# A two-block transformer on one core: the router's chain before the expert layer written in another order

## The chip, the cores and the metric

The kernel runs on one core of a Trainium2 chip, in one launch. The metric is device time in microseconds (us), the median of several executions. Below, PE is TensorE, DVE is VectorE, ACT is ScalarE, POOL is GpSimd and SP is SyncE, whose queue issues the weight transfers.

## What is computed

Two transformer blocks over 256 tokens of width 1024, in float32. The change lies in the first block's last layer, a hierarchical mixture of 16 experts in 4 groups:

```python
p_group = softmax(tf @ w_rg + b_rg); g_val, g_idx = top_k(p_group, 1)
in_group = e_logits[its group]; e_val, e_idx = top_k(in_group, 2)
weights = g_val * softmax(e_val)
for e in range(N_EXPERTS):
    hidden = silu(t @ w_gate[e]) * (t @ w_up[e])
    y = y + gate[:, e] * (hidden @ w_down[e])
```

Here t is the normed token. The second block then modulates its norms with shifts and scales that are products of a 1024 x 6144 matrix with a vector (w_mod); these products are the "modulation tiles" below.

## The kernel before, in words

Every float32 product is made of three float32r matmuls: a value is held as a high part (its float32r copy) and a low part (what the copy left out), and high x high, low x high and high x low are added up in PSUM. Weights come from HBM as pieces of 128 x 1024 (512 KB), in one long stream that SP issues in order into a ring of four slots (later in the layer four side slots as well). For each piece ACT copies the high part (wh, line 734, function split), DVE subtracts it (wl, line 2020), and PE waits for the low part (semaphore w_lo). SP issues a piece when DVE is done with the one that held its slot. Every engine runs its own list in the order written; nothing is scheduled.

The expert layer starts with the routing chain. PE makes the 20 logits (few_rows), DVE scales them and adds the bias (lines 2281, 2282), PE turns them (turn_logits, line 1566), and DVE finds each token's group (line 2312 to 2318, semaphore rt_group). PE counts the tokens of each group (rt_count), ranks them (rt_rank) and turns the norm's roots (rt_root); one semaphore, rt_counted, stands for all three. From the counts DVE finds the leading group (line 2334 and on) and writes the address of its weights (first_i, semaphore moe_first); SP reads it and only then issues the layer's first weights. DVE goes on with the two best experts, each token's place in its group's queue (dest, line 2358) and the weights of the gates (rt_gate, line 2371). Meanwhile PE turns the tokens themselves, to have them by token (turn_tokens): per chunk of 128 x 512, eight matmuls against the identity add high and low part in one PSUM bank; ACT copies the bank as uh (line 918), and DVE later subtracts uh from the bank to get ul (line 2376, turned_rest). At the end of this part PE multiplies ones, eight times (spin, line 1299, turn_over): it keeps PE busy and leaves no result that is used.

The leading group's four experts then run over all 256 tokens as eight half experts ("unit" jobs, functions gate_up and down: 24 matmuls of 128 x 256 for each of gate, up and down); the other three groups run over at most 128 gathered tokens each, twelve experts ("crowd" jobs, 36 matmuls of 128 x 512 each). The list SEQ mixes them: units 0 to 3 are jobs 0 to 3, then four times three crowd jobs and a unit, so that units are also jobs 7, 11, 15 and 19. In the loop over jobs PE first makes the next job's gate and up, then this job's down product. The first unit also waits for the squares of the context rows' norm (norm("ctx")), the gates (gate_full, gate_set), the clearing of the four sum banks (moe_cleared) and the slots of the crowd tokens (spread_slots).

Six modulation tiles, each two DVE operations of 128 x 1024 (mod_tiles, line 2148), are spread over the units 1 to 6 (MOD_UNIT), that is jobs 1, 2, 3, 7, 11 and 15: each stands ahead of the low part of that unit's hidden values (hidl, line 2440), which the down product waits for. POOL loads the matrix tiles, two ahead. What stands on DVE between the gates' weights and the first low part of weights is this:

```python
for c in range(4):
    turned_rest(c)
add_squares("ctx", 512)
```

## Time and profile before

| | |
|---|---|
| median of 3 executions | 1562.03 us (1559.44 to 1562.79) |
| the profiled execution | 1556.72 us, span 1554.9 us |
| PE busy | 1473.3 us, 95% of the span |
| DVE, ACT busy | 1058.3 us (68%), 758.5 us (49%) |
| mean granted TensorE clock | 0.989 |
| weight transfers | 512 KB a piece, HBM 163 GB/s over the span |

The span is the time from the first to the last instruction of the profiled execution; its own time has 1.8 us around it. PE is busy nearly throughout, so what an edit is worth has to be read from the places where PE stands still.

### The profile page before, as it was taken

The page shows a single profiled execution, that of the slowest core. Times are in us where ns is not written, and L with a number is a line of the kernel's source. Part 1 is how long each engine was busy: PE and PEld are TensorE (multiplying, and loading weights), DVE is VectorE, ACT ScalarE, POOL GpSimd, SP SyncE. Part 2 cuts the span into 40 slices and gives each one's busy share as a digit, 9 for nine tenths or more (in the row PEclk, how much of TensorE's full clock was granted, in tenths as well). Part 3 has the DMA queues.
Part 4 walks back from the last instruction along what each step waited for, and adds up shares of the span by engine and source line. Part 5 has one row for each costly group of instructions (what it writes and reads, how often), then busy time and mean ns, then how long its engine had stood idle before and what let it go on. Part 6 is the DMA issues. An engine that isn't in the chain of part 4 may idle for free.

```text
span 1554.9 us, 24439 instructions
## 1 busy us (share of the span) xinstructions
PE 1473.3 (95%) x8792; PEld 1261.4 (81%) x8792; DVE 1058.3 (68%) x1805; ACT 758.5 (49%) x1293; POOL 94.0 (6%) x167
## 2 busy tenths in 40 slices
PE   7999999699998999997999999999999998999997
PEld 7999698698777877655878888888877966899997
DVE  5877496668888899258687765554579736665554
ACT  5544554346666635346435421443235546574562
POOL 0010000000000000003001100000000002000000
PEclk9999999899999999999999999999999999999999
DMA  8676263249987435403336764555433331356562
GB/s 322 219 272 188 81 187 112 84 148 332 318 284 242 127 120 189 114 14 69 133 114 208 248 203 148 170 194 163 150 124 111 121 94 29 99 173 189 176 185 85
DMA packets 87123, 254.22 MB, mean 163 GB/s; under 512 B 7904, under 2 KB 31600, under 8 KB 86912
## 3 DMA queue, kind: packets, MB, share of 16 engines
q1 hardware_dynamic: 69264, 188.70, 36.8%
q0 software_dynamic: 17776, 64.41, 14.0%
q8 instruction: 53, 0.87, 0.2%
q14 instruction: 30, 0.25, 0.0%
HBM read 251.99 MB, written 1.09 MB: 163 GB/s over the span
## 4 chain that ended last, share of the span: by engine, by line
PE 82%; DVE 10%; ACT 3%; issue 3%; DMA 1%; SPq 0%; DVEq 0%; ACTq 0%
PE pair L1255 80%; DVE wl L2020 1%; DVE sq L2679 1%; PE pair L1299 1%; ACT wh L734 1%; DVE uv L2056 1%; DVE sq L2096 1%; DVE small L2088 1%; PE pair L1444 1%; DMA uv<-in_w_stream 1%; ACT wh L724 0%; DVE spent L2148 0%; DVE uh_f L2148 0%; ACT sq L796 0%; DMA table<-in_table 0%
## 5 line engine op out<-in xcount | busy, mean ns | idle before, releaser
L1255 PE MATMUL pair<-uh,wh 128*128 128x256 f32 (+3 forms) x1280 | 415.8, 325 | 5.4 <-DVE ul L2047 2.8
L1255 PE MATMUL pair<-ul,wh 128*128 128x256 f32 (+3 forms) x1280 | 412.3, 322 | 0.0
L1255 PE MATMUL pair<-uh,wl 128*128 128x256 f32 (+3 forms) x1280 | 411.2, 321 | 0.0
L2020 DVE TENSOR_TENSOR wl<-ring,wh 128x1024 fp32r<-128x1024 f32 x190 | 229.5, 1221 | 58.5 <-ACT wh L734 55.3
L1255 PEld LDWEIGHTS pair<-uh,wh 128*128 128x128 f32 (+1 forms) x1280 | 235.2, 184 | 32.6 <-issue 6.8
L1255 PEld LDWEIGHTS pair<-uh,wl 128*128 128x128 f32 (+1 forms) x1280 | 235.3, 184 | 23.4
L1255 PEld LDWEIGHTS pair<-ul,wh 128*128 128x128 f32 (+1 forms) x1280 | 235.1, 184 | 22.3
L734 ACT ACTIVATE wh<-ring 128x1024 fp32r<-128x1024 f32 x186 | 193.7, 1053 | 81.2 <-PE pair L1255 61.8
L2013 DVE TENSOR_TENSOR wl<-ring,wh 128x1024 fp32r<-128x1024 f32 x120 | 146.8, 1224 | 108.3 <-ACT wh L724 105.0
L724 ACT ACTIVATE wh<-ring 128x1024 fp32r<-128x1024 f32 x124 | 130.4, 1052 | 158.8 <-PE pair L1255 158.8
L1255 PE MATMUL pair<-hh,wh 128*128 128x512 f32 (+1 forms) x512 | 172.5, 337 | 1.8 <-DVE res L2856 1.8
L1255 PE MATMUL pair<-hl,wh 128*128 128x512 f32 (+1 forms) x512 | 172.2, 336 | 0.0
L1255 PE MATMUL pair<-hh,wl 128*128 128x512 f32 (+1 forms) x512 | 170.7, 333 | 0.0
L1255 PEld LDWEIGHTS pair<-hh,wh 128*128 128x128 f32 x512 | 96.1, 188 | 14.2 <-issue 2.5
L1255 PEld LDWEIGHTS pair<-hh,wl 128*128 128x128 f32 x512 | 96.2, 188 | 10.8
L1255 PEld LDWEIGHTS pair<-hl,wh 128*128 128x128 f32 x512 | 96.0, 188 | 9.5
L1209 ACT ACTIVATE sq<-pair 128x512 f32<-128x512 f32 (+1 forms) x64 | 31.3, 489 | 107.4 <-PE pair L1255 105.6
L2821 DVE TENSOR_TENSOR hl<-sq,hh 128x512 f32 (+1 forms) x64 | 35.7, 558 | 69.5 <-ACT hh L1214 69.5
L2133 DVE CUSTOM_DVE_ANT_0 mod_w<-mod_w,mod_c 128x1024 f32<-128x1024 f32 x56 | 68.3, 1220 | 0.0
L640 POOL DMA_DIRECT2D mod_w<-in_mods x67 | 35.4, 529 | 477.4 <-DVE macc L2133 313.9
L1255 PE MATMUL pair<-wh,uh 128*128 128x256 f32 (+1 forms) x192 | 57.5, 300 | 3.0 <-ACT qkp L1042 3.0
L1255 PE MATMUL pair<-wh,ul 128*128 128x256 f32 (+1 forms) x192 | 57.4, 299 | 0.0
(384 smaller groups left out, 2545.5 us busy)
## 6 DMA issues: line engine op xcount, KB each, us to landing
ring<-in_w_stream SPq DMA_DIRECT2D x310, 512.0 KB, 4.3
mod_w<-in_mods POOLq DMA_DIRECT2D x67, 512.0 KB, 3.9
uh_side<-in_w_stream SPq DMA_DIRECT2D x20, 512.0 KB, 5.9
uv<-in_w_stream SPq DMA_DIRECT2D x20, 512.0 KB, 5.8
uh_f<-in_mods POOLq DMA_DIRECT2D x18, 512.0 KB, 4.9
qk_w<-in_mods POOLq DMA_DIRECT2D x6, 512.0 KB, 6.4
in_w<-in_mods POOLq DMA_DIRECT2D x5, 512.0 KB, 3.9
uv<-c_rows POOLq DMA_DIRECT2D x4, 512.0 KB, 7.6
```

Source lines behind the costliest of these rows:

```text
L640: pool.dma_start(dst, src).then_inc(S(f"mod_in{g % 2}"), 16)
L724: act.activation(wh[:, s, :], ring[:, s, :], ACT.Copy).then_inc(S("w_hi"), 1)
L734: act.activation(part_of(wh, n), staged(n), ACT.Copy).then_inc(S("w_hi"), 1)
L1209: act.activation(r, bank[(b0 + j) % 4][:, 0:n], ACT.Relu).then_inc(S("job_emptied_act"), 1)
L1255: ins = pe.matmul(*operands, **flags)
L1299: pe.matmul(bank[b], spin[:, 0:P], spin[:, :], start=True, stop=True)
L1444: last = pe.transpose(bank[6][:, to * P:(to + 1) * P], prob[i % 2][:, j * P:(j + 1) * P], ident)
L2013: tt(wl[:, s, :], ring[:, s, :], wh[:, s, :].bitcast(F32), ALU.subtract).then_inc(S("w_lo"), 1)
L2020: tt(part_of(wl, n), staged(n), part_of(wh, n).bitcast(F32), ALU.subtract).then_inc(S("w_lo"), 1)
L2056: last = stt(o, src, g, r, ALU.mult, ALU.mult)
L2133: return dve.tensor_tensor_reduce(out=mod_w[l][k], in0=mod_w[l][k], in1=mod_c[l][which], scale=1.0, scalar=0.0, op0=ALU.mult, op1=ALU.add, ...
L2821: tt(hl[:, d, 0:n].rearrange("p a b -> p (a b)"), sq[:, 2 + j % 2, 0:n], hh[:, d, 0:n].rearrange("p a b -> p (a b)").bitcast(F32), ALU.sub ...
```

## The change

The routing chain is written in another order, and two things are computed otherwise:

- DVE does the constants (count_up, route, a zeroed tile, the modulation's sums) before it waits for the logits.
- The tokens are turned as eight chunks, four of the high part and four of the low part, with four matmuls each; ACT copies all eight out of PSUM as uh and ul. DVE's subtraction (turned_rest) is gone.
- PE counts the groups ahead of chunk 3; rt_counted stands for the counts alone, and ranks and roots get a semaphore of their own (rt_ranked). PE's spin has 12 matmuls and stands behind the ranks.
- ACT makes the first weight piece's high part ahead of the context's last square; DVE adds the squares and makes the first low part right behind dest, ahead of the gates' weights. PE does norm("ctx") ahead of the first unit.
- The gates are scaled by the root while they are still one value a token, and ACT copies them out of PSUM; DVE multiplied them by the root before. The clearing of the sum banks moves behind spread_slots.
- The six modulation tiles stand in jobs 1, 3, 5, 9, 13 and 17 (MOD_JOBS): two units, and one crowd job out of each three; each stands behind the low part hidl of its job.

```diff
@@ -126 +126 @@
-MOE_SPIN = 8
+MOE_SPIN = 12
@@ -220,2 +220,2 @@
-MOD_UNIT = (0, 1, 1, 1, 1, 1, 1, 0)
-MOD_IN = MOD_MOE + sum(MOD_UNIT)
+MOD_JOBS = (1, 3, 5, 9, 13, 17)
+MOD_IN = MOD_MOE + len(MOD_JOBS)
@@ -443 +443,2 @@
-        turn_banks = [bank[JOBS.number("moe_y", 0) % 4], bank[JOBS.number("moe_y", 1) % 4], bank[6], bank[7]]
+        turn_banks = [bank[JOBS.number("moe_y", j) % 4] for j in range(3)] + [bank[6], bank[7], bank[5], bank[4]]
+        turn_banks.append(turn_banks[0])
@@ -916 +917 @@
-for c in range(4):
+for c in range(8):
@@ -918,2 +919,2 @@
-    act.activation(tok_chunk(uh, c), turn_banks[c][:, :].rearrange("p (a t) -> p a t", a=2),
-                   ACT.Copy).then_inc(S("turned_hi"), 1)
+    act.activation(tok_chunk(uh if c < 4 else ul, c % 4), turn_banks[c][:, :].rearrange("p (a t) -> p a t", a=2),
+                   ACT.Copy).then_inc(S("turned"), 1)
@@ -929 +929,0 @@
-square("ctx", 3, res[:, 6:8, CTX], P, 512)
@@ -931 +931,2 @@
-split(S_MOE + 2)
+split(S_MOE)
+square("ctx", 3, res[:, 6:8, CTX], P, 512)
@@ -933 +934 @@
-split(S_MOE + 4)
+split(S_MOE + 2)
@@ -951,0 +953,6 @@
+        if i == 0:
+            act.wait_ge(S("gate_full"), 1)
+            for j in range(2):
+                act.activation(gates[:, 2 * j:2 * j + 2, :], gate_banks[j][:, :].rearrange("p (a t) -> p a t", a=2),
+                               ACT.Copy).then_inc(S("gate_set"), 1)
+            split(S_MOE + 3)
@@ -955 +962 @@
-        split(last + 3 if i else 0)
+        split(last + 3)
@@ -1572 +1579 @@
-    if c == 3:
+    if c == 4:
@@ -1573,0 +1581,2 @@
+    if c == 7:
+        pe.wait_ge(S("turned"), 1)
@@ -1575,4 +1584,3 @@
-        f, tok = 4 * (c % 2) + j, slice(c // 2 * P, c // 2 * P + P)
-        o = turn_banks[c][:, j * P:(j + 1) * P]
-        mm(o, fh[:, f, tok], ident_r[:, :], start=True, stop=False)
-        last = mm(o, fl[:, f, tok], ident_r[:, :], start=False, stop=True)
+        f, tok = 4 * (c % 2) + j, slice(c % 4 // 2 * P, c % 4 // 2 * P + P)
+        last = mm(turn_banks[c][:, j * P:(j + 1) * P], (fh if c < 4 else fl)[:, f, tok], ident_r[:, :],
+                  start=True, stop=True)
@@ -1585 +1592,0 @@
-turn_tokens(3)
@@ -1589 +1596,5 @@
-    mm(rt_count, tab("nones"), ones_g[:, b, :], start=(b == 0), stop=(b == 1))
+    last = mm(rt_count, tab("nones"), ones_g[:, b, :], start=(b == 0), stop=(b == 1))
+last.then_inc(S("rt_counted"), 1)
+for c in range(3, 8):
+    turn_tokens(c)
+pe.wait_ge(S("moe_first"), 1)
@@ -1595,2 +1606,3 @@
-last.then_inc(S("rt_counted"), 1)
-turn_over(MOE_SPIN, 5)
+last.then_inc(S("rt_ranked"), 1)
+pe.wait_ge(S("turned"), 2)
+turn_over(MOE_SPIN, JOBS.number("moe_y", 1) % 4)
@@ -1627,0 +1640,2 @@
+pe.wait_ge(S("turned"), 8)
+norm("ctx", P, T)
@@ -1630,2 +1643,0 @@
-pe.wait_ge(S("turned_lo"), 4)
-norm("ctx", P, T)
@@ -1638,6 +1650,10 @@
-pe.wait_ge(S("moe_zero"), 1)
-pe.wait_ge(S("gate_set"), 1)
-for b in y_banks:
-    for k in range(2):
-        mm(b[:, k * T:(k + 1) * T], hidl[:, 1, 0:P], uh[:, k, LAT], start=(k == 0), stop=False,
-           skip_group_check=True).then_inc(S("moe_cleared"), 1)
+
+def clear_sums():
+
+    pe.wait_ge(S("moe_zero"), 1)
+    pe.wait_ge(S("gate_set"), 2)
+    for b in y_banks:
+        for k in range(2):
+            mm(b[:, k * T:(k + 1) * T], hidl[:, 1, 0:P], uh[:, k, LAT], start=(k == 0), stop=False,
+               skip_group_check=True).then_inc(S("moe_cleared"), 1)
+
@@ -1710,0 +1727 @@
+        clear_sums()
@@ -2279,4 +2295,0 @@
-dve.wait_ge(S("rt_logits"), 1)
-dve.wait_ge(S("norm_rstd"), NORM["ffn"] + 1)
-ch.link(tt(logit_rows[0:20, :], rt_bank[0:20, 0:T], rstd[0:20, 0:T], ALU.mult))
-ts(logit_rows[0:20, :], logit_rows[0:20, :], tab("b_route", 20), None, ALU.add).then_inc(S("rt_rows"), 1)
@@ -2290 +2303,13 @@
-
+ts(hidl[:, 1, 0:P], ones, 0.0, None, ALU.mult).then_inc(S("moe_zero"), 1)
+ts(eps2, tab("eps"), EPS, None, ALU.mult).then_inc(S("eps2_set"), 1)
+dve.wait_ge(S("mod_used"), MOD_MOE)
+ch.link(tt(modv[:, 0:32], modv[:, 0:32], tab("b_mod")[:, 0:32], ALU.add))
+ch.link(stt(gmod[:, 0, :], modv[:, 16:32], 1.0, tab("g1_0"), ALU.add, ALU.mult))
+ch.link(tt(gcomb.rearrange("p (k o) -> p k o", o=1),
+           gmod[:, 0, :].rearrange("p (k o) -> p k o", o=2)[:, :, 0:1],
+           tab("g_fin1").rearrange("p (k o) -> p k o", o=1), ALU.mult))
+dve.memset(modv[:, 2 * N_MOD:4 * N_MOD], 0.0).then_inc(S("macc_out"), 1)
+dve.wait_ge(S("rt_logits"), 1)
+dve.wait_ge(S("norm_rstd"), NORM["ffn"] + 1)
+ch.link(tt(logit_rows[0:20, :], rt_bank[0:20, 0:T], rstd[0:20, 0:T], ALU.mult))
+ts(logit_rows[0:20, :], logit_rows[0:20, :], tab("b_route", 20), None, ALU.add).then_inc(S("rt_rows"), 1)
@@ -2353,0 +2379 @@
+dve.wait_ge(S("rt_ranked"), 1)
@@ -2358,0 +2385,3 @@
+add_squares("ctx", 512)
+lo_end[0] = N_PIECES
+split(S_MOE)
@@ -2367 +2396 @@
-tt(tok_v[:, :, 0:4], tmp, over(root_of), ALU.mult)
+tt(tok_v[:, :, 0:4], tmp, over(root_of), ALU.mult).then_inc(S("tok_v"), 1)
@@ -2371,13 +2400,2 @@
-tt(lead_w, tmp, over(lone), ALU.mult).then_inc(S("rt_gate"), 1)
-
-def turned_rest(c):
-
-    dve.wait_ge(S("turned_hi"), c + 1)
-    tt(tok_chunk(ul, c), turn_banks[c][:, :].rearrange("p (a t) -> p a t", a=2),
-       tok_chunk(uh, c).bitcast(F32), ALU.subtract).then_inc(S("turned_lo"), 1)
-
-for c in range(4):
-    turned_rest(c)
-add_squares("ctx", 512)
-ts(hidl[:, 1, 0:P], ones, 0.0, None, ALU.mult).then_inc(S("moe_zero"), 1)
-lo_end[0] = N_PIECES
+dve.wait_ge(S("tok_v"), 1)
+tt(lead_w, tok_v[:, :, 0:4], over(lone), ALU.mult).then_inc(S("rt_gate"), 1)
@@ -2384,0 +2403,4 @@
+for b in range(TB):
+    last = ts(pick[:, b, :], count_up[:, :], dest[:, b, :], None, ALU.is_equal)
+last.then_inc(S("pick_set"), 1)
+split(S_MOE + 2)
@@ -2391,22 +2412,0 @@
-ts(eps2, tab("eps"), EPS, None, ALU.mult).then_inc(S("eps2_set"), 1)
-dve.wait_ge(S("mod_used"), MOD_MOE)
-ch.link(tt(modv[:, 0:32], modv[:, 0:32], tab("b_mod")[:, 0:32], ALU.add))
-ch.link(stt(gmod[:, 0, :], modv[:, 16:32], 1.0, tab("g1_0"), ALU.add, ALU.mult))
-ch.link(tt(gcomb.rearrange("p (k o) -> p k o", o=1),
-           gmod[:, 0, :].rearrange("p (k o) -> p k o", o=2)[:, :, 0:1],
-           tab("g_fin1").rearrange("p (k o) -> p k o", o=1), ALU.mult))
-dve.memset(modv[:, 2 * N_MOD:4 * N_MOD], 0.0).then_inc(S("macc_out"), 1)
-split(S_MOE + 2)
-scale_gate(0)
-dve.wait_ge(S("gate_full"), 1)
-for j in range(2):
-    last = tt(gates[:, 2 * j:2 * j + 2, :], gate_banks[j][:, :].rearrange("p (a t) -> p a t", a=2),
-              rstd[:, 0:T].rearrange("p (a t) -> p a t", a=1).to_broadcast([P, 2, T]), ALU.mult)
-last.then_inc(S("gate_set"), 1)
-for b in range(TB):
-    last = ts(pick[:, b, :], count_up[:, :], dest[:, b, :], None, ALU.is_equal)
-last.then_inc(S("pick_set"), 1)
-split(S_MOE + 4)
-dve.wait_ge(S("gate_set"), 1)
-dve.wait_ge(S("moe_cleared"), 8)
-
@@ -2427,3 +2427,2 @@
-        if i:
-            scale_gate(i)
-            split(last + 2)
+        scale_gate(i)
+        split(last + 2)
@@ -2430,0 +2430,2 @@
+        if i == 0:
+            dve.wait_ge(S("gate_set"), 2)
@@ -2435,0 +2437,2 @@
+        if i == 1:
+            dve.wait_ge(S("moe_cleared"), 8)
@@ -2438 +2440,0 @@
-        mod_tiles(MOD_UNIT[n], spent[:, :, :])
@@ -2440,0 +2443 @@
+        mod_tiles(int(i in MOD_JOBS), spent[:, :, :])
@@ -2461,0 +2465 @@
+    mod_tiles(int(i in MOD_JOBS), spent[:, :, :])
```

How it moves PE's list, from the turned logits to the first weights (pair is PSUM, fh and fl are the tokens' parts, small holds the groups, sq the context's squares). Before:

```order
L1566 MATMUL pair<-table,logit_rows 128x20 [waits rt_rows]
...
L1255 MATMUL pair<-ident_r,fh 128x128 [waits norm_rstd]
...
L1255 MATMUL pair<-small,table 128x4 [waits rt_group]
L1255 MATMUL pair<-small,table 128x4 x4
L1255 MATMUL pair<-table,rstd 128x1 x2
L1299 MATMUL pair<-spin 128x512 x8
L1255 MATMUL pair<-fh,wh 128x256 [waits w_lo]
```

and now:

```order
L1573 MATMUL pair<-table,logit_rows 128x20 [waits rt_rows]
...
L1262 MATMUL pair<-small,table 128x4 [waits rt_group]
...
L1262 MATMUL pair<-ident_r,fl 128x128 [waits norm_rstd]
...
L1262 MATMUL pair<-small,table 128x4 [waits moe_first]
L1262 MATMUL pair<-small,table 128x4 x2
L1262 MATMUL pair<-table,rstd 128x1 x2
L1306 MATMUL pair<-spin 128x512 [waits turned]
L1306 MATMUL pair<-spin 128x512 x11
L1262 MATMUL pair<-sq,table 128x256 [waits norm_add,turned]
...
L1262 MATMUL pair<-fh,wh 128x256 [waits w_lo]
```

The two count matmuls stand ahead of most of the turning, the ranks behind it, and the context's norm (sq) stands ahead of the first weights.

DVE's list from dest (the reduce into route) to the first low part of weights. Before:

```order
L2358 TENSOR_REDUCE route<-route 128x2 [waits dve_step]
L2360 SCALAR_TENSOR_TENSOR small<-small 128x2 [waits rt_exp]
...
L2371 TENSOR_TENSOR route<-small,route 128x8 [waits dve_step]
L2376 TENSOR_TENSOR ul<-pair,uh 128x2x256 [waits turned_hi] x4
L2034 TENSOR_TENSOR sq<-sq 128x512 [waits norm_sq]
...
L2020 TENSOR_TENSOR wl<-ring,wh 128x1024 [waits w_hi] x2
```

and now:

```order
L2384 TENSOR_REDUCE route<-route 128x2 [waits dve_step]
L2051 TENSOR_TENSOR sq<-sq 128x512 [waits norm_sq,dve_step]
L2051 TENSOR_TENSOR sq<-sq 128x512 [waits norm_add,norm_sq]
L2037 TENSOR_TENSOR wl<-ring,wh 128x1024 [waits w_hi]
L2389 SCALAR_TENSOR_TENSOR small<-small 128x2 [waits rt_exp]
...
L2401 TENSOR_TENSOR route<-route 128x8 [waits tok_v,dve_step]
```

The gates' weights moved behind the first piece, and the subtraction into ul is not there any more.

DVE's list in job 5, a crowd job, from the low part of its hidden values. Now:

```order
L2464 TENSOR_TENSOR hidl<-pair,hidh 128x256 [waits crowd_hi]
L2165 ISA spent,modv<-uh_f_123,uv 128x1024 [waits mod_used,mod_in0]
...
L2165 ISA uh_f_123,modv<-uh_f_123,uv 128x4x256
...
L2037 TENSOR_TENSOR wl<-uh_side,wh 128x1024 [waits w_hi]
```

A modulation tile (the two ISA rows) stands between hidl and the next low part of weights, where nothing stood before.

## Rows read from the trace of the kernel before

**Rows 1.** The page's chain that ended last, by engine.
```profile
PE 82%; DVE 10%; ACT 3%; issue 3%; DMA 1%; SPq 0%; DVEq 0%; ACTq 0%
```
**Rows 2.** Timeline of PE in routing: start, us, engine, line, instruction, count [idle before].
```profile
291.35 1.23 PE L1255 MATMUL pair<-small,table 128*128 128x4 f32 x10
...
292.88 2.10 PE L1299 MATMUL pair<-spin 128*128 128x512 f32 x8
306.02 0.58 PE L1255 MATMUL pair<-fh,wh 128*128 128x256 f32 x1 [11.04 <-DVE wl L2020]
...
314.01 1.89 PE L1255 MATMUL pair<-sq,table 128*128 128x256 f32 x8
315.74 1.95 PE L1255 MATMUL pair<-table,route 128*128 128x128 f32 x16
319.16 1.19 PE L1255 MATMUL pair<-uh,hidl 128*128 128x256 f32 x8 [1.47 <-DVE gates L2403]
...
325.63 0.60 PE L1255 MATMUL pair<-table,route 128*128 128x128 f32 x4
```
**Rows 3.** Stretches of 1 us: PE, PEld, DVE, ACT, POOL busy; clock; DMA share; GB/s.
```profile
297.00:298.00 1.00, 0.00 (x0) 0.00 (x0) 0.86 (x5) 0.00 (x0) 0.00 (x0) 0.68 0.93 377
309.00:310.00 1.00, 1.00 (x6) 1.00 (x6) 0.00 (x0) 0.00 (x0) 0.00 (x0) 0.50 0.94 340
```
**Rows 4.** Timeline of DVE in the routing chain.
```profile
287.98 0.41 DVE L2281 TENSOR_TENSOR logit_rows<-pair,rstd 20x256 f32<-20x256 f32 x1 [3.20 <-ACT rstd L767]
...
289.92 0.19 DVE L2312 COPY small<-pair 128x40 f32<-128x40 f32 x1
...
290.94 0.17 DVE L2318 TENSOR_TENSOR small<-small 128x8 f32<-128x8 f32 x1
...
293.06 0.16 DVE L2334 TENSOR_REDUCE route<-pair 128x1 f32<-128x4 f32 x1 [1.22 <-PE pair L1255]
...
298.26 0.16 DVE L2358 TENSOR_REDUCE route<-route 128x2 f32<-128x8 f32 x1
...
299.96 2.48 DVE L2376 TENSOR_TENSOR ul<-pair,uh 128x512 fp32r<-128x512 f32 x4
302.36 1.48 DVE L2034 TENSOR_TENSOR sq<-sq 128x512 f32<-128x512 f32 x2
```
**Rows 5.** Timeline of ACT and of SP's queue there, and the transfers' landing times.
```profile
289.34 1.06 ACT L918 ACTIVATE uh<-pair 128x512 fp32r<-128x512 f32 x2
...
303.13 0.63 ACT L754 ACTIVATE sq<-res 128x512 f32<-128x512 f32 x1 [6.20 <-DVE sq L2034]
...
295.02 34.40 SPq L606 DMA_DIRECT2D ring<-in_w_stream  x11
...
DMA to landing us min/median/max: 3.5/4.3/6.8
```
**Rows 6.** Timelines of DVE, ACT and PE in job 7, a unit with a tile.
```profile
389.61 1.22 DVE L2148 CUSTOM_DVE_ANT_1 spent<-uh_f,uv 128x1024 f32<-128x1024 f32 x1
...
390.05 1.04 ACT L734 ACTIVATE wh<-ring 128x1024 fp32r<-128x1024 f32 x1
...
393.51 0.50 PE L1255 MATMUL pair<-wh,xgh 128*128 128x512 f32 x1 [2.43 <-DVE wl L2020]
```
**Rows 7.** Timelines of DVE and PE in the crowd jobs 9 and 13.
```profile
414.33 2.35 DVE L2020 TENSOR_TENSOR wl<-ring,wh 128x1024 fp32r<-128x1024 f32 x2
...
416.49 0.39 PE L1255 MATMUL pair<-wh,hidh 128*128 128x512 f32 x1
...
450.99 0.42 DVE L2461 TENSOR_TENSOR hidl<-pair,hidh 128x256 fp32r<-128x256 f32 x1
...
454.07 0.40 PE L1255 MATMUL pair<-wh,hidh 128*128 128x512 f32 x1
```
**Rows 8.** Who waited for whom, 320 to 500 us: total, times, longest.
```profile
SPq L606 <- DVE wl L2020: 117.1, 79, 11.3
...
ACT wh L734 <- DMA ring<-in_w_stream: 4.0, 6, 3.0
```

More of the change, by code:

```diff
@@ L928, in _ @@
             ch.link(act.activation(gsum, gsum, ACT.Exp, scale=0.5))
+            hi_end[0] = N_PIECES
+            split(S_MOE)
             square("ctx", 3, res[:, 6:8, CTX], P, 512)
-            hi_end[0] = N_PIECES
+            root("ctx", P, T, D, rstd[:, T:2 * T])
             split(S_MOE + 2)
-            root("ctx", P, T, D, rstd[:, T:2 * T])
-            split(S_MOE + 4)
             def gathered(f):
```

## The prediction

> **What bounds the kernel now.** I read the chain that ended last first: PE makes up 82% of it, DVE 10% [rows 1]. PE is the bound, and time is to be found only where PE stands still or runs slowly. So next I went through the timeline of PE for its idle places. Two lie in the routing part [rows 2]: after the last spin matmul, at 294.98, PE does nothing for 11.04 us until the first weights' low part (wl) is there at 306.02, and it waits 1.47 us for the gates at 319.16. The clock comes on top: the granted clock falls during that idle stretch, between 297 and 298, where its mean is 0.68 (2.4 GHz, then 1.2), and at 309, with PE busy again, it still stands at 0.50, 1.2 GHz [rows 3]. The 48 matmuls of the first unit take 7.99 us (306.02 to 314.01); the next unit's 48, from 320.2 to 325.63, take 5.43 [rows 2]. The slow clock thus costs 2.5 us. Third, I followed DVE back from 306.02 [rows 4]: the counts arrive at 293.06, after a wait of 1.22; dest is done at 298.42; the gates' weights follow; then the four subtractions into ul (2.48 us) and the two additions of squares (1.48 us). ACT's last square of the context had waited 6.20 us for these additions and stands ahead of the first weight copy [rows 5]. The weights had been on their way since 295.02 and were no longer the last thing waited for.
>
> Later there are three waits of the kind at 393.51: PE stands 2.43 us for a low part in job 7, and DVE spends two operations of 1.14 on a modulation tile just ahead of it [rows 6]. The trace has this pattern three times, in jobs 7, 11 and 15.
>
> **The routing part, worked forward.** All times are on the trace's clock.
>
> Counts. PE's first two chunks now take 8 matmuls of 0.11 us in place of 16, so PE is free when the logit rows are ready. These start at 287.98 [rows 4]; with 0.41 for each of two such operations and about 0.35 for the two transposes and their landing (an estimate: the counting matmuls take 0.22 each, 1.53 us for seven between 291.35 and 292.88 [rows 2]) the copy starts at 289.15, against 289.92 behind the constants: 0.77 earlier. The constants themselves move into DVE's wait of 3.20 us ahead of the logits; they add up to some 2.4 us and cost nothing there. If that cover were short, each 0.2 us too much would delay all that follows. The group is known at 290.94 + 0.17 - 0.77 = 290.34, two counting matmuls take 0.44, and with 0.2 for the landing the counts are there at 291.0. DVE itself is done with what stands ahead of them at 293.06 - 1.22 - 0.77 = 291.07. The counts are thus read at 291.1, 1.96 us earlier.
>
> Weights. SP's first issue moves with it from 295.02 to 293.06, and with the shortest landing of 3.5 us [rows 5] the first piece is there at 296.56. ACT must have its eight copies behind it: 0.53 each from 289.34 [rows 5] with a short wait for PE's counts, done at 294.1, and the exponentials until 295.7. It makes the high part from 296.6 to 297.65 (1.04 [rows 6]) and then the square (0.63 [rows 5]) until 298.3.
>
> DVE. dest is done at 298.42 - 1.96 = 296.46, the squares are added by 297.95, and the first low part takes 1.22 more, until 299.2. The 2.48 us of subtraction are gone; ACT's four added copies are 2.1 us, and they are over before the landing, which covers them.
>
> PE. After the counts, 20 turning matmuls until 293.05, five small ones until 294.15, twelve spins of 0.26 until 297.3. The context's norm starts at 297.95, when the squares are added, and takes 315.74 - 314.01 = 1.73 us: 299.7. The gap of 0.65 us ahead of it is far shorter than the idle time of over 2 us before the clock fell [rows 2, 3], so I take 2.4 GHz. The first half of the unit ends at 299.7 + 2.72 = 302.4 (24 of the 48 in 5.43). Its second piece is late next: ACT does the norm's root before it (two operations, taken as 0.9 with their landing), then high part 1.05 and low part 1.22, 303.1; PE waits 0.7 and ends at 305.8. The gates' matmuls take 1.85 [rows 2], until 307.65; the next unit's first half until 310.4. Its second piece now stands on ACT behind the two copies of the gates (0.53 each, from 307.85): high part at 310.0, low part at 311.25, a new wait of 0.85. PE gets to spread_slots at 314.0 where it was at 325.63 [rows 2]. The clearing, 1.03 us, comes after it now. **The routing part gives 11.6 - 1.0 = 10.6 us.** All later issues of weights hang on DVE's low parts (SP waited 117.1 us for them, ACT 4.0 us for ring transfers [rows 8]), so the later stages move along.
>
> **The modulation tiles.** In jobs 7, 11 and 15 the low part PE waits for could start when its high part is ready, 390.05 + 1.04 = 391.1, in place of 392.24 behind the tile [rows 6]. That gives 1.12 each, 3.4 us; the rest of the wait stays, as ACT and DVE still hand the values to and fro. In the crowd jobs DVE has less room. In job 9 the tile takes the place of the low part at 414.33: that one then starts at 416.61 and is done at 417.83, while PE wants it at 416.49: a new wait of 1.4 us [rows 7]. In job 13 hidl is issued at 450.99; 0.34 + 2.28 + 1.22 later it is 454.83, and PE wants it at 454.07: 0.8 us [rows 7]. I take job 5, where the transfers run close, like job 9 and job 17 like job 13: 4.4 us for the four. In job 3 DVE now waits for ACT's copy before the tile, 0.5 us that the tile covered before. **The tiles cost 4.4 + 0.5 - 3.4 = 1.5 us.** Bounds: nothing new to wait for (a gain of 3.4) and all four paid in full (4 x 2.28 + 0.5 - 3.4, a loss of 6.2). I take the worked value, which lies nearest to the two jobs read.
>
> **Sum.** -10.6 + 1.5 = -9.1 us. The profiled execution took 1556.72 us with a span of 1554.9, so a like one would take 1547.6. The median of the runs is 5.3 us above the profiled execution; on that scale it is 1562.03 - 9.1 = 1552.9. A measurement here tells a difference from none at about 0.2%, 3.1 us.
>
> **Rivals.**
> 1. *The tiles are paid in full.* DVE has six low parts of 1.22 in each crowd job, so a delay may not be made up before the next unit. Against it: in jobs 9 and 13 DVE is 0.9 and 1.4 us ahead of PE [rows 7]. -10.6 + 6.2 = -4.4: 1557.6.
> 2. *The tiles are hidden*, because PE's wait in one job gives DVE room in the next: -14.0, 1548.0. The two jobs in rows 7 speak against it.
> 3. *The clock falls all the same.* The spin ends at 297.3, and a slip of the squares or the landing lengthens the gap. Price: 2.5 us less the 0.7 wait it swallows: 1554.7.
> 4. *The counts don't come earlier*, so the change doesn't do what it says: SP reads the address a whole 1 us after it is written, and if that or the landing sets the start, PE begins at 301.1, 1.4 us later: 1554.3.
> 5. *The transfers take over, and it is slower.* SP issues strictly in order behind DVE's low parts [rows 8]; a tile in a crowd job holds SP for 2.28 us, just where three jobs in four want six pieces each. It decides when less than 2.28 us of transfers are queued at that moment. Then each tile is lost to the stream, 9.1 us; the stream's start gains only the 1.96 of the first issue, PE's other gains end in waits for transfers, and one modulation load moves from the units into the crowds, 512 KB at the 377 GB/s of [rows 3], an estimate of 1.4 us: -2.0 + 9.1 + 1.4 = +8.5, 1570.5. For it: ACT did wait for ring transfers, 3.0 us once [rows 8]. Against it: that is 4.0 us in 180, and landings of 4.3 us [rows 5] mean about three pieces under way. The Trainium skill (Trainium Kernel Development and Optimization, Key Constraints) says that transfers issued by SP, ACT and POOL share the same 16 DMA engines and interleave; by that rule alone the moved load would take its 1.4 us from the weights, 1554.3 in all. No wait of ACT in rows 8 can be put down to such a load.
>
> **Numbers.** The forecast has a chance of 0.64, with a range of its own of 1550.5 to 1556; rivals 1 to 5 have 0.09, 0.08, 0.08, 0.06 and 0.05. The range of 1548.0 to 1558.0 leaves out rival 5, the far side of rivals 1 and 2 and a spread of the executions of some 2 us. Faster by over 0.2%: the forecast and rivals 2 to 4 and half of rival 1 give 0.90; I take off 0.03 for that spread: 0.87. Within 0.2%: the other half of rival 1 and that 0.03, 0.08. Slower: 0.05.
>
> **What would show it.** Right: the counts read near 291.1, SP's first issue near 293.1, the context's norm near 298 and the first unit near 299.7 at a clock of 1.00; two short waits of PE (0.7 and 0.85) in place of 1.47; in jobs 7, 11, 15 waits of about 1.3 in place of 2.43, and new ones of 0.8 to 1.4 in jobs 5, 9, 13, 17. Wrong: a gap of over 2 us between spin and norm, ACT's first high part later than 297 for another reason than the landing, or waits of ACT for the ring that run through the crowd jobs.

## The result and the profile after

The changed kernel takes 1549.1 us in the median of five executions (1547.81 to 1552.2); the kernel before, run beside it, takes 1560.12 (1556.92 to 1562.79). The ratio is 0.9942, with a 95% interval of 0.9923 to 0.9961. A second comparison, further down, gives 0.9951 (0.9934 to 0.9967). So the change saves 5 to 12 us. The forecast of 1552.9 was counted from a median before of 1562.03; counted from 1560.12 it would be 1551.0. It has the sign and about the size, and 1549.1 lies in the range of 1548.0 to 1558.0, though below the forecast's own 1550.5 to 1556. The stages say how much of it is the change's own, and there the sum is less good than its total.

The profiled execution took 1547.81 us, with a span of 1546.0. PE's share of the chain that ended last falls from 82% [rows 1] to 76%, and DVE's rises:

```profile
PE 76%; DVE 12%; ACT 4%; issue 4%; DMA 3%; DVEq 0%; SPq 0%; ACTq 0%
```

The timeline of PE in the routing part, which answers to [rows 2] (start, us, engine, line, instruction, count, idle time before it):

```profile
289.61 0.61 PE L1262 MATMUL pair<-small,table 128*128 128x4 f32 x4 [0.69 <-DVE small L2343]
...
294.21 5.40 PE L1306 MATMUL pair<-spin 128*128 128x512 f32 x12
299.45 1.89 PE L1262 MATMUL pair<-sq,table 128*128 128x256 f32 x8
...
304.57 0.39 PE L1262 MATMUL pair<-fh,wh 128*128 128x256 f32 x1 [0.40 <-DVE wl L2037]
307.50 1.94 PE L1262 MATMUL pair<-table,route 128*128 128x128 f32 x16
312.83 0.39 PE L1262 MATMUL pair<-fh,wh 128*128 128x256 f32 x1 [0.55 <-DVE wl L2037]
315.77 0.60 PE L1262 MATMUL pair<-table,route 128*128 128x128 f32 x4
317.47 1.20 PE L1262 MATMUL pair<-uh,hidl 128*128 128x256 f32 x8
```

The idle stretch of 11.04 us and the wait for the gates are gone. PE goes from the spins straight into the context's norm and the first unit, then waits 0.40 and 0.55 us for two low parts. The row at 315.77 is spread_slots, the one at 317.47 the clearing that now stands behind it. But twelve spins take 5.24 us (294.21 to 299.45), 0.44 each where [rows 2] had 0.26. The stretches of 1 us that answer to [rows 3] say why (PE, PEld, DVE, ACT, POOL busy; granted clock; DMA share; GB/s):

```profile
292.00:293.00 1.00, 1.00 (x10) 1.00 (x9) 0.83 (x6) 1.00 (x3) 0.00 (x0) 0.79 0.00 0
293.00:294.00 1.00, 1.00 (x7) 1.00 (x6) 0.83 (x7) 1.00 (x7) 0.00 (x0) 0.50 0.72 139
...
299.00:300.00 1.00, 1.00 (x5) 0.82 (x4) 0.69 (x6) 0.00 (x0) 0.00 (x0) 0.80 0.63 111
```

The granted clock falls to 0.50, 1.2 GHz, at 292.6, with PE shown busy 1.00 for 3.0 us before that (since 289.61). It comes back at 299.4. DVE, ACT and SP did what was forecast. These rows answer to [rows 4] (DVE) and [rows 5] (ACT, and SP's queue):

```profile
287.18 0.41 DVE L2314 TENSOR_TENSOR logit_rows<-pair,rstd 20x256 f32<-20x256 f32 x1 [1.11 <-ACT rstd L768]
...
290.26 0.16 DVE L2359 TENSOR_REDUCE route<-pair 128x1 f32<-128x4 f32 x1
...
295.47 0.16 DVE L2384 TENSOR_REDUCE route<-route 128x2 f32<-128x8 f32 x1
295.67 1.49 DVE L2051 TENSOR_TENSOR sq<-sq 128x512 f32<-128x512 f32 x2
297.08 1.22 DVE L2037 TENSOR_TENSOR wl<-ring,wh 128x1024 fp32r<-128x1024 f32 x1
...
291.25 2.06 ACT L919 ACTIVATE ul<-pair 128x512 fp32r<-128x512 f32 x4
...
295.92 1.06 ACT L735 ACTIVATE wh<-ring 128x1024 fp32r<-128x1024 f32 x1 [1.30 <-DMA ring<-in_w_stream]
...
292.22 36.72 SPq L607 DMA_DIRECT2D ring<-in_w_stream  x13
```

Everything here starts 0.80 us earlier than before (logit rows at 287.18, in [rows 4] at 287.98), so I count from the logit rows. The counts are read 3.08 us behind them (forecast 3.12), SP issues at 5.04 (5.08), ACT begins the first high part at 8.74 (8.6), the squares are added at 9.98 (9.97), the first low part is done at 11.12 (11.22).

In the expert layer PE's waits in the jobs with moved tiles and in job 7 answer to [rows 6, 7]; here are jobs 5, 7, 9 and 13, and DVE's rows in job 7:

```profile
372.22 0.50 PE L1262 MATMUL pair<-wh,hidh 128*128 128x512 f32 x1 [1.58 <-DVE wl L2037]
...
385.93 0.50 PE L1262 MATMUL pair<-wh,xgh 128*128 128x512 f32 x1 [1.33 <-DVE wl L2037]
...
410.32 0.50 PE L1262 MATMUL pair<-wh,hidh 128*128 128x512 f32 x1 [1.24 <-DVE wl L2037]
...
447.80 0.50 PE L1262 MATMUL pair<-wh,hidh 128*128 128x512 f32 x1 [0.64 <-DVE wl L2037]
...
383.70 0.43 DVE L2442 TENSOR_TENSOR hidl<-eg,hidh 128x256 fp32r<-128x256 f32 x1 [0.48 <-ACT hidh L964]
384.65 1.23 DVE L2037 TENSOR_TENSOR wl<-ring,wh 128x1024 fp32r<-128x1024 f32 x1 [0.52 <-ACT wh L735]
```

Job 7 waits 1.33 in place of 2.43, as jobs 11 and 15 do; jobs 5, 9, 13 and 17 (0.65) wait anew. ACT's waits for transfers, [rows 8], hardly moved (who waited for whom, 310 to 490 us: total, times, longest):

```profile
ACT wh L735 <- DMA ring<-in_w_stream: 5.0, 5, 3.2
```

### Where the 8.9 us of the two profiled executions came from

I cut both traces at three rows that stand in each: DVE's logit rows, PE's spread_slots, and PE's first matmul behind its last wait of the layer, which before and after is this row:

```profile
503.60 0.39 PE L1255 MATMUL pair<-hidh,wh 128*128 128x256 f32 x1 [1.61 <-DVE hidl L2440]
```
```profile
497.23 0.39 PE L1262 MATMUL pair<-hidh,wh 128*128 128x256 f32 x1 [1.61 <-DVE hidl L2442]
```

| stretch | before | after | difference |
|---|---|---|---|
| up to the logit rows | 287.98 | 287.18 | -0.80 |
| logit rows to spread_slots | 37.65 | 28.59 | -9.06 |
| spread_slots to the layer's end | 177.97 | 181.46 | +3.49 |
| from there to the end of the span | 1051.3 | 1048.8 | -2.5 |

The clearing, 1.03 us, crossed the second cut. So the routing gave 8.0 and the tiles took 2.5: 5.6 us. The last stretch is the same code in both kernels: up to PE's last matmul it is 5632 matmuls before and after. These rows hold the busy time and the clock of that stretch, first of the kernel before, then of the changed one:

```profile
503.60:1547.80 1044.20, 1009.19 (x5632) 842.94 (x5632) 683.18 (x1184) 485.21 (x867) 71.05 (x130) 0.99 0.45 139
```
```profile
497.23:1538.88 1041.65, 1004.12 (x5632) 839.34 (x5632) 683.27 (x1184) 485.12 (x867) 71.08 (x130) 1.00 0.45 139
```

Within them the clock stood at 1.2 GHz for 17.1 us before and for 6.8 after, 10.2 less, and PE was busy 5.1 us less, half of that. Against it PE stood still 2.5 us longer (1041.65 - 1004.12 = 37.5, before 35.0), and no run shows why. So nothing shows that the 2.5 us of this stretch are the change's; the clock accounts for more than they are.

### The profile page after: what moved, and what is told of

Its sections match the earlier page's. It is cut to its first block, busy times and chain, and to the rows that moved or that the text cites. A ratio compares the mean times of both kernels' runs of the same rounds, so it can differ in the third digit from the quotient of the medians.

```text
span 1546.0 us, 24449 instructions
## 1 busy us (share of the span) xinstructions
PE 1471.3 (95%) x8796; PEld 1258.1 (81%) x8796; DVE 1054.8 (68%) x1799; ACT 761.5 (49%) x1299; POOL 94.1 (6%) x167
## 4 chain that ended last, share of the span: by engine, by line
PE 76%; DVE 12%; ACT 4%; issue 4%; DMA 3%; DVEq 0%; SPq 0%; ACTq 0%
PE pair L1262 74%; DVE wl L2037 2%; DMA mod_w<-in_mods 2%; ACT wh L735 1%; PE pair L1306 1%; DMA uh_side<-in_w_stream 1%; DVE sq L2683 1%; DVE uv L2073 1%; DVE sq L2113 1%; DVE small L2105 1%; DVE mod_w L2150 1%; ACT wh L725 1%; PE pair L1451 1%; DVE spent L2165 1%; DVE uh_f L2165 1%
```

## The experiments

Each kernel was run in five rounds beside the kernel before, four or three kernels on one chip at a time. The intervals of the ratios are 0.3 to 0.5% wide, so the stages of the traces decide most questions; they are set side by side behind the last experiment.

**1. Work in PE's two waits.** The first theory was that the clock fell because PE had stood still for 0.36 and 0.69 us.

```diff
 turn_tokens(1)
+turn_over(1, 5)
 turn_logits()
 turn_tokens(2)
+turn_over(2, 5)
 pe.wait_ge(S("rt_group"), 1)
```

> The changed kernel with three more spin matmuls in PE's two waits of the routing chain: one ahead of turn_logits (PE stood 0.36 us there), two ahead of the wait for the groups (0.69 us). Theory A (the granted clock fell at 292.8 because PE had stood still and done short work from 287 to 290): the clock stays at 1.00, the twelve spins take 3.1 us in place of 5.4, the context's norm starts when the squares are added, near 297.2 in place of 299.45, and spread_slots comes 2 us earlier: about 2 us faster than the changed kernel, ratio to before 0.993. Theory B (the clock falls for the small turning matmuls themselves, standing still has no part): the clock falls near 292.8 all the same, and the time is that of the changed kernel, or 0.2 us more for the spins.

Measured: 1549.86 us, ratio 0.9954 (0.9935 to 0.9973). One wait is gone and the other is 0.18 us; PE is busy 6.45 of the 6.70 us ahead of the fall. The clock falls all the same, and the twelve spins take as long (two timeline rows and two stretches of this kernel):

```profile
291.33 0.61 PE L1262 MATMUL pair<-small,table 128*128 128x4 f32 x4 [0.18 <-DVE small L2345]
...
295.51 5.47 PE L1306 MATMUL pair<-spin 128*128 128x512 f32 x12
```
```profile
288.00:294.70 6.70, 6.45 (x52) 5.67 (x51) 4.73 (x28) 6.01 (x13) 0.00 (x0) 1.00 0.00 0
295.00:296.00 1.00, 1.00 (x5) 0.99 (x5) 0.83 (x6) 0.97 (x8) 0.00 (x0) 0.50 0.50 152
```

It stands at 0.50 from 294.8 to 301.6; spread_slots comes 28.59 us behind the logit rows, exactly as without the three spins. So the fall does not need PE's two waits: theory B, as far as one execution goes.

**2. Five spins in place of twelve.**

```diff
-MOE_SPIN = 12
+MOE_SPIN = 5
```

> The changed kernel with 5 spins in place of 12. Theory A (the spins lie on the path once the clock has fallen): at 0.43 us each seven fewer end 3.0 us earlier, and the context's norm then starts when the squares are added, near 297.2 in place of 299.45. If the clock comes back as early as before, near 299.3, all of 2.2 us is kept until the first unit, and about 1.5 to 2 at spread_slots (the second piece's low part is next to be late). Rival: it is the twelve spins that bring the clock back; with five it comes back later, the first unit's half at 1.2 GHz costs up to 1.4 us more, and the gain is under 0.7 us or nothing.

Measured: 1548.63 us, ratio 0.9962 (0.9945 to 0.9979). The norm starts 11.29 us behind the logit rows, 1.0 earlier, but the clock is low from 291.4 to 301.7, and the norm's eight matmuls take 3.24 us:

```profile
299.06 3.24 PE L1262 MATMUL pair<-sq,table 128*128 128x256 f32 x8 [0.19 <-DVE sq L2051]
```

spread_slots comes 28.96 behind the logit rows, 0.37 later. Against that execution the rival has it: what fewer spins give, the slow unit takes. But the clock fell earlier here, 3.65 us behind the logit rows in place of 5.40. The two executions with twelve spins whose clock was low for 10.2 us as well (the changed kernel again and experiment 5, below) have spread_slots at 30.16 and 30.24, 1.2 later than here. So whether five spins are better or worse stays open.

**3. The tiles back in their old places.**

```diff
-MOD_JOBS = (1, 3, 5, 9, 13, 17)
+MOD_JOBS = (1, 2, 3, 7, 11, 15)
...
+                    mod_tiles(int(i in MOD_JOBS), spent[:, :, :])
                     dve.wait_ge(S("moe_hi"), n + 1)
...
-                    mod_tiles(int(i in MOD_JOBS), spent[:, :, :])
...
-                mod_tiles(int(i in MOD_JOBS), spent[:, :, :])
```

> The changed kernel with the six modulation tiles where they were: jobs 1, 2, 3, 7, 11 and 15, ahead of hidl. Theory A (the moved tiles cost more than they give): PE waits 2.4 in jobs 7, 11, 15 and no more than 0.4 in jobs 5, 9, 13, 17; the sum of PE's waits from the spread of the slots to the end of the layer falls by about 1 us from 11.96, and the time is 1 to 3 us below the changed kernel's. Rival (the tiles gain in their new place): the time is 1 to 3 us above it.

Measured: 1548.75 us, ratio 0.9948 (0.993 to 0.9967). The times cannot tell it from the changed kernel. The layer takes 179.63 us, 1.83 less, though this execution had the clock at 0.50 for 3.4 us within it (from 388.6), which the changed kernel's had not. Set beside the same matmuls of the kernel before, those 3.4 us delayed PE by 1.5. So between these two executions the moved tiles cost 1.8 us as measured, and 3.4 when that stretch is taken out. The six executions of the changed routing with the tiles in their new places lie between 180.70 and 182.17, so this price is good to about 1 us.

**4. The tiles' move alone**, in the kernel before.

```diff
-MOD_UNIT = (0, 1, 1, 1, 1, 1, 1, 0)
-MOD_IN = MOD_MOE + sum(MOD_UNIT)
+MOD_JOBS = (1, 3, 5, 9, 13, 17)
+MOD_IN = MOD_MOE + len(MOD_JOBS)
...
-                    mod_tiles(MOD_UNIT[n], spent[:, :, :])
                     dve.wait_ge(S("moe_hi"), n + 1)
...
+                    mod_tiles(int(i in MOD_JOBS), spent[:, :, :])
...
+                mod_tiles(int(i in MOD_JOBS), spent[:, :, :])
```

> The kernel before with the tiles' move alone, no change to the routing. Theory A: PE's waits in jobs 7, 11 and 15 go from 2.43 to about 1.3, new waits of 1.6, 1.2, 0.6 and 0.6 us come in jobs 5, 9, 13 and 17, and the whole costs 1 to 3 us against the kernel before, ratio 1.001 to 1.002. Rival (the tiles give 3.4 us or part of it): ratio 0.998 to 0.999, and the rest of the routing's gain is smaller than 8 us.

Measured: 1555.5 us, ratio 0.9998 (0.998 to 1.0016), which holds both theories. The trace shows the waits of theory A, job 9 first, then job 11:

```profile
419.06 0.50 PE L1255 MATMUL pair<-wh,hidh 128*128 128x512 f32 x1 [1.25 <-DVE wl L2020]
...
432.77 0.50 PE L1255 MATMUL pair<-wh,xgh 128*128 128x512 f32 x1 [1.33 <-DVE wl L2020]
```

The layer takes 180.52 us, 2.55 more than before, with the clock at full speed in both. That agrees with the 2.46 of the changed kernel (3.49 less the clearing). PE's idle time explains some 1.1 of it; the rest stands in PE's busy time, 167.06 us before and 168.46 here, as these two rows of the layer show (before, then this kernel):

```profile
325.63:503.60 177.97, 167.06 (x963) 143.34 (x961) 148.04 (x181) 112.45 (x139) 3.00 (x4) 1.00 0.82 278
```
```profile
325.43:505.95 180.52, 168.46 (x963) 143.24 (x961) 147.84 (x181) 112.45 (x139) 2.99 (x4) 1.00 0.81 274
```

The starts of the same 961 matmuls, set side by side, say where it goes. The four new waits are 1.29, 1.25, 0.64 and 0.64 us of idle time, 3.8 together, but what stands behind them starts 4.8 us later: each wait delays PE by some 0.25 us more than its idle time, 0.15 at the wait itself and 0.1 over the next matmuls. The waits in jobs 7, 11 and 15 give 3.3 back, low parts around jobs 3 and 4 come 0.8 later, and 0.2 is spread over the rest.

**5. Tiles where DVE is idle.** With the old places DVE stands still around hidl in the last crowd job ahead of each unit (timeline of DVE in job 10, kernel of experiment 3):

```profile
415.31 1.23 DVE L2037 TENSOR_TENSOR wl<-uv,wh 128x1024 fp32r<-128x1024 f32 x1
417.50 0.42 DVE L2464 TENSOR_TENSOR hidl<-pair,hidh 128x256 fp32r<-128x256 f32 x1 [0.97 <-ACT hidh L979]
419.81 0.42 DVE L2411 TENSOR_TENSOR eg<-pair,rstd 128x256 f32<-128x256 f32 x1 [1.89 <-PE pair L1262]
```

```diff
-MOD_JOBS = (1, 3, 5, 9, 13, 17)
+MOD_JOBS = (1, 2, 3, 6, 10, 14)
...
                 split(nxt[len(nxt) // 2 - 1] + AHEAD)
+                mod_tiles(int(i in MOD_JOBS), spent[:, :, :])
                 dve.wait_ge(S("crowd_hi"), n + 1)
...
```

The tile in a unit stands ahead of hidl, as in experiment 3.

> The changed kernel with three tiles ahead of hidl in units 1, 2, 3 (as before) and three ahead of hidl in the crowd jobs 6, 10 and 14, the last ones ahead of a unit. With the tiles in their old places DVE stood idle there for 0.97 us ahead of hidl (416.54 to 417.50) and 1.89 us behind it (417.92 to 419.81). Theory A (a tile costs what DVE has not idle): two operations of 1.14 fit into that, so PE waits 1.3 us in jobs 7, 11, 15 in place of 2.43, with no new wait in jobs 9, 13, 17; the stretch from spread_slots to the layer's end takes 176.3 us, 3.3 less than the 179.63 with the old places and 5 less than the 181.46 of the changed kernel. Rival (hidl, now 1.3 us later, is what PE waits for at the end of the unit's gate and up): a new wait of about 1 us each behind jobs 6, 10 and 14 and no gain over the old places.

Measured: 1547.41 us, ratio 0.9933 (0.9911 to 0.9956). The layer takes 175.34 us, 6.1 less than in the changed kernel and 4.3 less than in experiment 3, where 1.5 are that execution's clock. Job 11's wait is 1.32, and two of the three jobs have a small one for hidl (0.29 and 0.33):

```profile
421.71 0.50 PE L1262 MATMUL pair<-wh,xgh 128*128 128x512 f32 x1 [1.32 <-DVE wl L2037]
```

Theory A. The routing was slower in this execution, 30.24 us: the clock fell earlier, at 290.4, and came back at 300.7.

**6. A spin behind each of five turning chunks**, beside the three of experiment 1.

```diff
 for c in range(3, 8):
     turn_tokens(c)
+    if c == 6:
+        pe.wait_ge(S("turned"), 1)
+    if c == 7:
+        pe.wait_ge(S("turned"), 2)
+    turn_over(1, (5, 5, 4, JOBS.number("moe_y", 0) % 4, JOBS.number("moe_y", 1) % 4)[c - 3])
```

> The changed kernel with three spin matmuls in PE's two waits of the routing chain, as in the earlier run, and one more behind each of the five turning chunks that follow the counts; twelve at the end, as ever. Theory A (the clock falls while PE's matmuls are all short ones, whether it stands still or not, and work of 128 x 512 among them holds it): the granted clock stays at 1.00 to the first unit, the last twelve spins take about 3.1 us, the context's norm starts 10.0 to 10.5 us behind the logit rows in place of 12.27, and spread_slots comes about 26.5 us behind them in place of 28.59. Rival (the clock falls in this stretch anyway): it falls 4 to 6 us behind the logit rows, the spins take 5.2 us, and spread_slots is as late as in the changed kernel or up to 1 us later.

Measured: 1545.06 us, ratio 0.9936 (0.9914 to 0.9957). The clock stays at 1.00 all through (stretch, then PE's rows), and twelve spins take 2.83 us:

```profile
284.00:301.00 17.00, 16.74 (x110) 14.80 (x109) 13.83 (x70) 10.72 (x26) 0.00 (x0) 1.00 0.35 126
```
```profile
295.87 3.00 PE L1306 MATMUL pair<-spin 128*128 128x512 f32 x12
298.70 1.89 PE L1262 MATMUL pair<-sq,table 128*128 128x256 f32 x8
```

The norm starts 10.24 us behind the logit rows, spread_slots 26.55: 2.04 us of the routing, as theory A had it. The layer takes 182.17 us, 0.7 more than in the changed kernel: PE now waits for a low part in job 4, as ACT has to wait 2.48 us for that piece's transfer:

```profile
357.28 0.50 PE L1262 MATMUL pair<-wh,xgh 128*128 128x512 f32 x1 [1.52 <-DVE wl L2044]
```

**7. The counts behind the turning chunks again.**

```diff
-pe.wait_ge(S("rt_group"), 1)
...
-last.then_inc(S("rt_counted"), 1)
 for c in range(3, 8):
     turn_tokens(c)
-pe.wait_ge(S("moe_first"), 1)
+pe.wait_ge(S("rt_group"), 1)
+for b in range(TB):
+    mm(rt_count, tab("nones"), ones_g[:, b, :], start=(b == 0), stop=(b == 1))
...
-last.then_inc(S("rt_ranked"), 1)
+last.then_inc(S("rt_counted"), 1)
...
-dve.wait_ge(S("rt_ranked"), 1)
```

> The changed kernel with the counts behind the turning chunks again, in front of ranks and roots, one semaphore for all three. The counts are then read some 2.5 us later, and SP's first issue, the landing, dest and the squares with them. Theory A (the start of the first unit is set by the twelve spins on a slow clock, not by the counts): the context's norm starts 12.3 to 12.8 us behind the logit rows, as against 12.27, and the unit within 0.5 us of 13.8; spread_slots loses under 1 us. Rival (the counts set the start, as predicted: 1.96 us of the gain are theirs): the unit starts about 2 us later, near 15.8, and spread_slots near 30.5.

Measured: 1551.36 us, ratio 0.9964 (0.9943 to 0.9985). My theory A falls. The squares come so late that PE stands still behind the spins, and the clock, back at 1.00 since 296.9, falls again at 300.3:

```profile
301.27 3.75 PE L1262 MATMUL pair<-sq,table 128*128 128x256 f32 x8 [2.89 <-DVE sq L2049]
```

The first unit starts 16.02 us behind the logit rows, spread_slots comes at 31.35: 2.76 us later than in the changed kernel, 1.1 to 1.2 later than in the two executions whose clock was low as long (30.24 and 30.16). So the early counts are worth 1.1 to 2.8 us, which holds the 1.96 of the prediction.

**8. DVE's order alone**, in the kernel before: squares and first low part right behind dest.

```diff
-square("ctx", 3, res[:, 6:8, CTX], P, 512)
 hi_end[0] = N_PIECES
+split(S_MOE)
+square("ctx", 3, res[:, 6:8, CTX], P, 512)
 split(S_MOE + 2)
...
 ch.link(dve.tensor_reduce(dest, rank, AX_X, ALU.add))
+add_squares("ctx", 512)
+lo_end[0] = N_PIECES
+split(S_MOE)
...
-add_squares("ctx", 512)
...
-lo_end[0] = N_PIECES
```

> The kernel before with one part of the change alone: DVE adds the squares and makes the first low part right behind dest, ahead of the gates' weights and of the four subtractions, and ACT makes the first high part ahead of the context's last square. Worked from the rows of before: dest 298.42, squares 299.9, first low part 301.1, so the first unit starts 4.9 us earlier (13.1 us behind the logit rows in place of 18.04); its second piece's low part comes behind weights and subtractions near 306.5, about when the first half at 1.2 GHz is done. Theory A (most of the routing's gain is this order): spread_slots comes 4 to 5 us earlier, near 33 behind the logit rows in place of 37.65. Rival (it is the removed subtractions, 2.48 us, and the earlier counts that count): under 2.5 us, as the second piece, the gates and the clearing then wait for DVE.

Measured: 1554.79 us, ratio 0.9985 (0.9967 to 1.0004). The first unit starts 13.17 us behind the logit rows (13.1 expected), after a wait of 4.60 in place of 11.04, and spread_slots comes at 33.20: 4.45 earlier, over half of the routing's 8.0 (the clearing stands ahead of spread_slots here). A part may be the clock's, which was at 1.2 GHz for 10.2 us of the routing here and for 13.7 before.

```profile
300.44 0.58 PE L1256 MATMUL pair<-fh,wh 128*128 128x256 f32 x1 [4.60 <-DVE wl L2021]
```

The ratio is worth 2.3 us, and its interval holds 4.45 as well as nothing. In the profiled execution the clock stood at 0.50 twice within the layer, 6.8 us together; it took 180.66.

**9 to 11. The changed kernel again, both gains together, and ACT's order.** The second kernel has the edits of experiments 5 and 6. The third has two more:

```diff
+            split(S_MOE + 1)
             root("ctx", P, T, D, rstd[:, T:2 * T])
...
                     if i == 0:
+                        split(S_MOE + 3)
                         act.wait_ge(S("gate_full"), 1)
...
-                        split(S_MOE + 3)
```

> The changed kernel once more, beside the two versions below. Theory A (the change itself is worth 9.1 us in the routing, less 3.5 in the expert layer; the rest of the first difference came from stretches at the lower clock in code that is the same in both kernels): logit rows to spread_slots 28.6 us if the clock falls as it did, up to 30.5 if it stays down longer; spread_slots to the layer's end 181.4 to 181.5; ratio to before 0.995 to 0.997. Rival (the change is worth the 8.9 us of the first pair of profiled executions): ratio 0.994, with the later stages again 2.5 us shorter than those of before.

> The changed kernel with both edits that shortened a stage: the spins among the turning chunks, and the tiles in units 1, 2, 3 and the crowd jobs 6, 10 and 14, ahead of hidl. Theory A (the two stages do not touch each other): the granted clock stays at 1.00 through the routing, spread_slots 26.6 us behind the logit rows, 175.3 us from there to the layer's end, 201.9 together as against 210.05; 8 us faster than the changed kernel, ratio to before 0.990 to 0.992. Rival (the earlier start meets transfers that are not there yet): new waits of ACT for the ring in jobs 4 to 6, and the layer takes 177 us or more.

> The version with both edits, and ACT's order changed in two places: the second weight piece's high part ahead of the norm's root, the fourth's ahead of the two copies of the gates. Theory A (PE's waits of 0.40 and 0.55 us in the first two units are these two places): both waits go, spread_slots comes 0.95 us earlier, 25.6 behind the logit rows. Rival (the gates' copies, 1 us later, then hold eg and hidl of the first unit): PE waits for the first down product instead and the layer takes that much longer.

Measured: the changed kernel 1549.16 us, ratio 0.9951 (0.9934 to 0.9967); both edits 1539.45, ratio 0.9885 (0.9865 to 0.9906); with ACT's order 1540.13, ratio 0.9887 (0.9866 to 0.9908). The changed kernel's second ratio holds both theories. Its two stages are about those of theory A (30.16 and 180.83 us); behind the layer it was 8.5 us shorter than before, with no time at 1.2 GHz there, and not 2.5 as the rival had it. The gains add up: 202.33 us from the logit rows to the layer's end, a new wait of 1.02 in job 4 being the only loss. With ACT's order the two waits are gone and spread_slots comes 1.40 us earlier (0.95 expected), but the times of the last two kernels are the same within their intervals. The two waits are only 0.95 us of idle time. Here too a wait costs more than that: from the first unit's first matmul to the gates' matmuls it is 6.51 us with the wait of 0.40 and 5.84 without it (rows of the second kernel, then of the third), and from there to spread_slots 8.16 with the wait of 0.55 and 7.44 without.

```profile
301.32 0.47 PE L1262 MATMUL pair<-fh,wh 128*128 128x256 f32 x1
...
307.83 1.94 PE L1262 MATMUL pair<-table,route 128*128 128x128 f32 x16
```
```profile
299.01 0.47 PE L1263 MATMUL pair<-fh,wh 128*128 128x256 f32 x1
...
304.85 1.95 PE L1263 MATMUL pair<-table,route 128*128 128x128 f32 x16
```

The stages of all profiled executions, in us; the last column adds up the stretches at 1.2 GHz from the layer's end to PE's last matmul:

| kernel | logit rows to spread | spread to layer's end | at 1.2 GHz in routing | behind the layer |
|---|---|---|---|---|
| before | 37.65 | 177.97 | 13.7 | 17.1 |
| 4, tiles alone | 38.22 | 180.52 | 13.7 | 3.4 |
| 8, DVE's order alone | 33.20 | 180.66 | 10.2 | 17.1 |
| changed | 28.59 | 181.46 | 6.8 | 6.8 |
| changed, again | 30.16 | 180.83 | 10.2 | 0.0 |
| 1, spins in the waits | 28.59 | 181.41 | 6.8 | 20.5 |
| 2, five spins | 28.96 | 180.70 | 10.2 | 6.8 |
| 3, old tiles | 28.59 | 179.63 | 6.8 | 17.1 |
| 5, tiles in idle places | 30.24 | 175.34 | 10.2 | 10.2 |
| 6, spins between chunks | 26.55 | 182.17 | 0.0 | 6.8 |
| 7, counts late | 31.35 | 181.48 | 10.2 | 20.5 |
| 5 and 6 together | 26.46 | 175.87 | 0.0 | 20.5 |
| and ACT's order | 25.06 | 176.15 | 0.0 | 17.1 |

## Why the prediction was right, and where it was not

- **DVE, ACT and SP: right.** Counts, first issue, landing, squares and first low part came within 0.2 us of the forecast, counted from the logit rows. The constants, the copies of ul and the landing's cover cost nothing, as costed.
- **PE's clock: the step that failed.** The prediction let the spins end at 297.3 and took 2.4 GHz because the gap behind them is short. The clock fell ahead of the spins, with PE shown busy, and so the twelve spins ended at 299.45. Of rival 3 the outcome came true, by another way than its gap; its price was 1.8 us, and the clock cost 2.04 (28.59 less the 26.55 of experiment 6). The norm starts 2.3 us later than forecast, at 12.27 in place of 9.97, and spread_slots at 28.59 in place of 26.02. In experiment 6, with the clock held, norm, first unit and spread_slots come at 10.24, 11.78 and 26.55, within 0.6 us of the prediction's 9.97, 11.72 and 26.02. So the other steps of that sum hold to about 0.5 us. The routing's term was 8.0 for 10.6, and 2.0 of the 2.6 us missing are the clock's.
- **The two waits ahead of second pieces:** right in place, and experiment 11 shows that they were ACT's order. The idle time is 0.40 and 0.55 for 0.7 and 0.85, but the delay, which is what the sum used, is 0.67 and 0.72. The prediction's own terms for the first (299.7, 0.9, 1.05 and 1.22) add up to 302.9 and not to 303.1; that 0.7 came out nearly right is in part luck.
- **The tiles:** waits of 1.33 (about 1.3), 1.58 and 1.24 (1.4 each), 0.64 and 0.65 (0.8 each). Wait for wait the idle times were right, but the layer paid 2.5 us for 1.5 (3.4 against experiment 3 without its clock). The missing 1.0 is the forecast's second mis-sized term. By experiment 4 the four waits cost 4.8 for 4.4, low parts around jobs 3 and 4 0.8 for 0.5, and the three old waits give 3.3 for 3.4. Rival 2 (tiles hidden) is out by experiments 3 and 4, rival 1 (6.2 in full) as well.
- **Rival 4, counts not earlier:** out; the address is read as early as forecast, and experiment 7 prices it. **Rival 5, transfers take over:** out; ACT waited 5.0 us for the ring where [rows 8] have 4.0.
- **The total:** 9.1 us were forecast. The stages of the profiled pair give 5.6, the ratios 9.0 and 7.6 us with intervals that reach down to 6.1 and 5.1. The two misses, 2.6 and 1.0 us, both go against the change. In the first pair the 0.8 us ahead of the logit rows and the 2.5 behind the layer covered them, so that its 8.9 lies so near to 9.1 is luck. What lifts the medians over 5.6 is not shown; in the second comparison the mean granted clock was 0.991 over the changed kernel's executions and 0.988 over those of before, which goes the same way and is in part the routing's own.

The Trainium skill (TensorE: Matmul & The Clock Gate, HAM oscillation — how this bites in real kernels) has the clock fall through waits of PE. The idle stretch of [rows 2, 3] agrees with that. Experiment 1 does not: with PE busy 6.45 of the 6.70 us from 288 to 294.7 the clock fell too. The measurement decides. What it was instead is settled only in part: the clock fell in this place in all seven executions of changed routing without spins among the chunks, and in none of the three with them. Of the three kernels with PE's old order it fell there in one (experiment 8), so what tips it is not fixed by the program alone.

## What to carry to other kernels

A chain that ends in a wait of PE is worked out well from the timeline, row by row; the clock under it is a term of its own, and here it fell over short matmuls with PE hardly ever idle. A wait costs more than the idle time that the profile shows for it, here by some 0.2 us each; the starts of the same matmuls in two traces show it. Put movable work where the engine that does it is idle, not where the engine that waits has a gap: against their first place (179.0, the layer before with the clearing) the same six tiles cost 2.5 us in the changed kernel's and gave 3.7 (179.0 less 175.34) in the idle ones; counted from experiment 3 without its clock it is 3.4 and 2.8. When executions spread by more than the effect, cut the traces at rows that both have and compare stage by stage.

## What the hardware showed that was not expected

- The granted clock fell to 1.2 GHz with PE busy 1.00 for 3.0 us (the changed kernel) and for 6.45 of 6.70 us (experiment 1) in the profile's records, on 128 x 128 turning matmuls and matmuls of 4 columns or 1 (in experiment 1 with three spins of 128 x 512 early in that stretch). It stayed at 2.4 GHz in three of three executions with five spins of 128 x 512 among them, and three more ahead.
- Where it falls varies from execution to execution: 5.4 us behind the logit rows in the first profile of the changed kernel, 2.3 in the second, and the stretch at 1.2 GHz was 6.8 and 10.2 us.
- The spread between executions is largely the clock's: the code behind the layer, the same in all, took longest with 20.5 us at 1.2 GHz (1045.9 us from the layer's end to PE's last matmul, PE busy 1011.2, experiment 1) and was shortest with none (1035.7, PE busy 999.4, the changed kernel again).
